# Two token halves of a norm, taken apart: the order of the products at the seams between stages

## What is computed

```
h = x + gate * (hidden @ w_down)                       # the product that ends a stage
u = h * rsqrt(mean(h * h, axis=-1) + eps) * g + shift  # one number per token
y = u @ w_next                                         # the product that begins the next stage
```

## Time and profile before

| what | before |
|---|---|
| median of 3 runs | 3476.15 us (3474.97 to 3476.59) |
| profiled execution, first to last instruction | 3472.8 us |
| TensorE busy | 3406.4 us, 98% |
| VectorE busy | 2199.6 us, 63% |
| ScalarE busy | 600.3 us, 17% |
| mean granted clock of TensorE | 0.996 |

### The profile page before, as it was taken

The page is one execution under the profiler, slowest core; times in us unless marked ns, Lnnn a source line. Parts: engine busy times, 40 slices in busy tenths (PEclk is TensorE's granted clock), DMA queues, the critical chain, the costliest instruction groups (busy, mean ns, idle before and its releaser), DMA issues.

```text
span 3472.8 us, 40732 instructions
## 1 busy us (share of the span) xinstructions
PE 3406.4 (98%) x16336; PEld 2811.9 (81%) x16336; DVE 2199.6 (63%) x4356; ACT 600.3 (17%) x1260; POOL 10.6 (0%) x12
## 2 busy tenths in 40 slices
PE   8999999999999999999999999999999999999999
PEld 6888867768888888888578888877688866888888
DVE  7776858767767677565356545554346567677754
ACT  2000023331000010001331000023411244012100
POOL 0000000000000000000000000010000000000000
PEclk9999999999999999999999999999999999999999
DMA  6433412213434434332112222222222211222222
GB/s 254 156 135 141 181 64 88 91 41 127 149 122 159 164 140 153 112 114 83 51 49 74 94 87 79 91 87 70 67 75 85 84 67 61 85 80 91 85 79 79
DMA packets 62083, 355.72 MB, mean 102 GB/s; under 512 B 6292, under 2 KB 15124, under 8 KB 32276
## 3 DMA queue, kind: packets, MB, share of 16 engines
q1 hardware_dynamic: 61895, 353.12, 29.2%
HBM read 350.83 MB, written 9.34 MB: 104 GB/s over the span
## 4 chain that ended last, share of the span: by engine, by line
PE 87%; DVE 9%; issue 2%; DMA 1%; ACT 1%; DVEq 0%; SPq 0%; ACTq 0%
PE turn L424 37%; PE lin L424 29%; PE lin L366 4%; PE lin L476 4%; PE turn L366 3%; PE score L1435 2%; PE out L1464 1%; PE lin L473 1%; DMA normed_T<-in_ada 1%; DVE work L823 1%; PE turn L1449 1%; PE out L424 1%; DVE work L2888 1%; DVE normed_sums L567 1%; PE turn L476 1%
## 5 line engine op out<-in xcount | busy, mean ns | idle before, releaser
L424 PE MATMUL turn<-normed_sums,weight_ring 128*128 128x256 f32 x3712 | 867.6, 379 | 0.4 <-DVE small L2907 0.4
L424 PEld LDWEIGHTS turn<-normed_sums,weight_ring 128*128 128x128 f32 x3712 | 705.0, 190 | 96.8 <-DVE small L2907 0.8
L424 PE MATMUL lin<-normed_T,weight_ring 128*128 128x256 f32 x2096 | 479.9, 380 | 1.2 <-ACT normed_T L779 1.2
L424 PEld LDWEIGHTS lin<-normed_T,weight_ring 128*128 128x128 f32 x2096 | 397.6, 190 | 58.8 <-issue 5.2
L503 DVE TENSOR_TENSOR products<-products,lin 128x512 f32<-128x512 f32 x182 | 125.1, 687 | 406.9 <-PE lin L424 378.8
L424 PE MATMUL turn<-arena,weight_ring 128*128 128x256 f32 x1618 | 371.3, 379 | 0.6 <-DVE arena L567 0.6
L424 PE MATMUL lin<-arena,weight_ring 128*128 128x256 f32 x1608 | 364.7, 380 | 2.0 <-DVE weight_ring L535 1.6
L424 PE MATMUL lin<-normed_sums,weight_ring 128*128 128x256 f32 x1432 | 345.5, 380 | 4.1 <-DVE normed_sums L567 4.1
L424 PEld LDWEIGHTS lin<-arena,weight_ring 128*128 128x128 f32 x1608 | 304.4, 190 | 45.8 <-DVE weight_ring L535 3.3
L424 PEld LDWEIGHTS turn<-arena,weight_ring 128*128 128x128 f32 x1618 | 306.6, 190 | 42.3 <-issue 1.0
L424 PEld LDWEIGHTS lin<-normed_sums,weight_ring 128*128 128x128 f32 x1432 | 270.9, 190 | 44.1 <-issue 6.2
(11 more groups left out here) (329 smaller groups left out, 3363.4 us busy)
## 6 DMA issues: line engine op xcount, KB each, us to landing
weight_ring<-in_up SPq DMA_DIRECT2D x110, 1024.0 KB, 4.8
arena<-in_ada SPq DMA_DIRECT2D x54, 768.0 KB, 4.4
weight_ring<-in_down SPq DMA_DIRECT2D x40, 1024.0 KB, 5.0
normed_T<-in_ada SPq DMA_DIRECT2D x36, 768.0 KB, 4.6
weight_ring<-in_down SPq DMA_DIRECT2D x20, 768.0 KB, 4.3
weight_ring<-in_dil_qk SPq DMA_DIRECT2D x9, 1024.0 KB, 5.0
weight_ring<-in_hyb_qk SPq DMA_DIRECT2D x8, 1024.0 KB, 4.8
weight_ring<-in_xbc SPq DMA_DIRECT2D x6, 1024.0 KB, 5.0
```

What stands on the lines that cost most here:

```text
L424: last = pe.matmul(o[:, n * H:(n + 1) * H], weight_block(slot, pairs, block, kp), op(kind, kp0 + kp), start=opens and n == 0 and kp == kps ...
```

## The change

The last slab's order becomes a, b, c (t3 alone), e (t4), d (t1, b22). With e the first token half is complete, and d, which only the second half needs, runs behind it; in a down projection the d of the second chunk is held back too (its slot with it) and runs just ahead of the last chunk's d. Between these products TensorE makes the sums and the spread of the first half's norm, each half with a bank of its own. The next stage takes its first two slabs together (`arriving_pair_pe`): the first half's products b11 and b21 of slab 0, then those of slab 1, then the rest of slab 0 pair by pair, then the rest of slab 1. Between the first ones it makes the sums and the spread of the second half. VectorE scales half tiles, first those of the first half (`normed_dve`), with the last three residual adds of the second half (`late_adds_dve`) after two of them behind an output projection and after all eight behind a down projection; then the second half and the operand sums (`second_half_dve`). ScalarE shifts half tiles (`normed_act`). The hybrid stage does the same with its first two projections, the last norm writes its result in 16 halves, and ffn0, which begins the kernel, keeps the old form. The keep-busy products at the seams go.

```diff
-        LAST_GROUPS = "abcde"
-        LAST_PRODUCTS = {"d": ((6, "b22"),), "e": ((3, "t4"),)}
+        LAST_GROUPS = "abce"
+        LAST_PRODUCTS = {"c": ((2, "t3"),), "e": ((3, "t4"),), "d": ((4, "t1"), (6, "b22"))}
...
+        PAIR_RINGS = ((0, 1, 0, 4), (2, 3, 4, 0), (1, 2, 3, 0))
+
+        def arriving_pair_pe(pe, c, op, beside):
+            there = halves_there(pe, c)
+            slots = [take_summed(pe, c), c.n["slab"] % SLOTS]
+            for n in range(2):
+                if n == 1:
+                    pe.wait_ge(slot_full[slots[1]], 16 * (c.n["slab"] // SLOTS + 1))
+                for b in PAIR_RINGS[n][:2]:
+                    after(pe, lin_taken[b], c[f"bank{b}"])
+                first, second = (lin[b][:, 0:H] for b in PAIR_RINGS[n][:2])
+                for kp in range(4):
+                    for o, block, kind in ((first, 0, "b11"), (second, 1, "b21")):
+                        there(kind, kp)
+                        last = pe.matmul(o, weight_block(slots[n], 4, block, kp), op(kind, kp), start=kp == 0, stop=kp == 3,
+                                         skip_group_check=True)
+                        if kp == 3 and kind == "b11":
+                            last.then_inc(lin_full[PAIR_RINGS[n][0]], 1)
+                        beside()
+            c.banks(*PAIR_RINGS[0])
+            job_done(c)
+            after(pe, lin_taken[0], c["bank0"])
+            after(pe, lin_taken[4], c["bank4"])
+            banks = {"b": lin[1], "c": lin[0], "d": lin[4]}
+            for kp in range(4):
+                for g, n, block, kind in (("b", 1, 5, "t2"), ("c", 0, 4, "t1"), ("c", 1, 2, "t3"), ("d", 0, 6, "b22"),
+                                          ("d", 1, 3, "t4")):
+                    weights_there(pe, c, block, kp)
+                    there(kind, kp)
+                    last = pe.matmul(banks[g][:, n * H:(n + 1) * H], weight_block(slots[0], 4, block, kp), op(kind, kp),
+                                     start=kp == 0 and n == 0 and g != "b", stop=kp == 3, skip_group_check=True)
+                    if kp == 3 and n == 1:
+                        bank_close(c, last)
+            halves_seen(c)
+            take_summed(pe, c)
+            c.banks(*PAIR_RINGS[1])
+            job_done(c)
+            for kp in range(4):
+                weights_there(pe, c, 5, kp)
+                last = pe.matmul(lin[3][:, H:T], weight_block(slots[1], 4, 5, kp), op("t2", kp), start=False, stop=kp == 3,
+                                 skip_group_check=True)
+            bank_close(c, last)
+            for g in "cd":
+                product_group(pe, c, slots[1], 4, g, op)
+            c.banks(*PAIR_RINGS[2])
...
+        def first_half_norm_pe(pe, c, final=False):
+            done = itertools.count(1)
+            def beside():
+                i = next(done)
+                if i == 3:
+                    tail_sum_pe(pe, c, 1, final)
+                elif final and i == 12:
+                    second_spread_pe(pe, 0)
+                elif not final and i == 6:
+                    spread_half_pe(pe, c, 0)
+            return beside
...
+        def second_half_norm_pe(pe, c):
+            done = itertools.count(1)
+            def beside():
+                i = next(done)
+                if i == 5:
+                    second_half_sums_pe(pe, c)
+                elif i == 8:
+                    spread_half_pe(pe, c, 1)
+            return beside
...
+        def late_adds_dve(v, c, inst):
+            b = c["late_bank"]
+            o = lin[b]
+            v.wait_ge(lin_full[b], c[f"bank{b}"])
+            v.wait_ge(dve_step, c["late"])
+            add_to_tail(v, inst, 7, 1, o[:, 0:H]).then_inc(tail_ready, 1)
+            vlink(v, c, add_to_tail(v, inst, 6, 1, o[:, 0:H]))
+            add_to_tail(v, inst, 6, 1, o[:, H:T]).then_inc(lin_taken[b], 1)
...
+        LATE_ADDS = {"slab": 2, "chunks": KT}
+        LATE_ROOT = {"slab": 6, "chunks": KT}
+
+        def normed_dve(v, c, prev, scale_half, ahead=4):
+            what, inst, sums_ahead = prev
+            reciprocal_dve(v, c, 0)
+            if sums_ahead:
+                weight_sums(v, c, 3)
+            half_there(v, c)
+            for k in range(KT + 1):
+                if k == LATE_ADDS[what]:
+                    late_adds_dve(v, c, inst)
+                if k == LATE_ROOT[what]:
+                    reciprocal_dve(v, c, 1)
+                if k < KT:
+                    scale_half(0, k)
+            half_there(v, c)
+            second_half_dve(v, c, lambda k: scale_half(1, k), ahead)
...
             for g in LAST_GROUPS:
-                if g == "d":
+                if g == "c":
                     tail_sums_start_pe(pe, c)
                 elif g == "e":
                     tail_sum_pe(pe, c, 0)
                 product_group(pe, c, slot, 4, g, op, last_slab=True)
-            tail_sums_pe(pe, c)
+            product_group(pe, c, slot, 4, "d", op, last_slab=True, beside=first_half_norm_pe(pe, c))
...
+            beside = first_half_norm_pe(pe, c, final)
+            last = product_group(pe, c, held, 4, "d", hidden_op, kp0=4, opens=False, closes=False, last_slab=True,
+                                 beside=beside)
+            last.then_inc(chunk_used, 1)
+            product_group(pe, c, slot, 3, "d", hidden_op, kp0=8, opens=False, last_slab=True, beside=beside)
```

More of the change, by code:

```diff
@@ L587, in tiles_seen, with halves_there, there, halves_seen @@
             c.add("sums", 3 * KT // 2)
+        def halves_there(pe, c):
+            tiles0, sums0 = c["u"], c["sums"]
+            def there(kind, kp):
+                if kind in ("b11", "b21"):
+                    pe.wait_ge(u_ready, tiles0 + 2 * kp + (1 if kind == "b11" else 2))
+                elif kind != "b22":
+                    pe.wait_ge(sums_made, sums0 + 3 * kp + {"t1": 1, "t3": 1, "t2": 2, "t4": 3}[kind])
+            return there
+        def halves_seen(c):
+            c.add("u", 2 * KT)
+            c.add("sums", 3 * KT // 2)
         u_pairs = in_pairs(uT)
@@ L631, in spread_half, with rinv_half, spread_half_pe @@
             return ins
+        rinv_bank = (outp[1], outp[0])
+        def rinv_half(h):
+            return rinv_bank[h][:, 0:H]
+        def spread_half_pe(pe, c, h):
+            c.add("spread")
+            pe.wait_ge(rinv_ready, c["spread"])
+            for b in range(2):
+                ins = pe.transpose(rinv_bank[h][:, b * P:(b + 1) * P], roots[h][:, b:b + 1].to_broadcast([P, P]), C("ident"))
+            ins.then_inc(rinv_spread, 1)
         def spread_pe(pe, c):
@@ L670, in tail_act, with late_squares_act, add_to_tail, sums @@
                 product_step_act(s, c, g)
[L671 to L678, removed]
-        def tail_dve(v, c, inst, ahead=True):
[L682 to L689, removed]
+            for n in range(2):
+                c.add("tail")
+                s.wait_ge(tail_ready, c["tail"])
+                tail_square_act(s, c, n, final)
+            root_act(s, c, 0)
+        def late_squares_act(s, c, final=False):
+            c.add("tail")
+            s.wait_ge(tail_ready, c["tail"])
+            tail_square_act(s, c, 2, final)
+            c.wait_mark(s, "blocks")
+            tail_square_act(s, c, 3, final)
+        def add_to_tail(v, inst, m, h, src):
+            tile = half(hT[:, m, :], h)
+            if inst is None:
+                return v.tensor_tensor(tile, src, tile, ALU.add)
+            return v.scalar_tensor_tensor(out=tile, in0=src, scalar=gate[:, inst, m:m + 1], in1=tile, op0=ALU.mult,
+                                          op1=ALU.add)
+        def tail_dve(v, c, inst, ahead=True):
+            def sums(stage):
                 if ahead:
-                    for stage in stages:
-                        weight_sums(v, c, stage)
+                    weight_sums(v, c, stage)
             job_done(c, note="p1_there")
@@ L775, in ada_norm_act, with ada_norm_dve, shift_half @@
+        def ada_norm_dve(v, c, inst, prev):
+            normed_dve(v, c, prev, lambda h, k: v.scalar_tensor_tensor(
+                out=half(uT[:, k, :], h), in0=half(hT[:, k, :], h), scalar=gs[:, inst, k:k + 1], in1=rinv_half(h),
+                op0=ALU.mult, op1=ALU.mult).then_inc(scaled, 1))
+        def ada_norm_act(s, c, inst, prev, first_copy=True):
             layer, sub = inst // 3, inst % 3
-            for k in range(KT):
+            def shift_half(h, k):
                 c.add("scaled")
@@ L778, in ada_norm_act @@
                 s.wait_ge(scaled, c["scaled"])
[L779 to L785 removed]
+                tile = half(uT[:, k, :], h)
@@ L2090, in mla_units, with mla @@
             return units
-        def mla():
+        def mla(prev):
             def sp(e, c):
-                for n in range(3):
-                    load_pair(e, c, a["mla_down"][n])
+                load_arriving_pair(e, c, a["mla_down"][0], a["mla_down"][1])
+                load_pair(e, c, a["mla_down"][2])
                 skip_jobs(c)
```

(14 more changed lines are left out.)

353 lines of the change are left out of this document (223 added, 130 removed).

## The result

The changed kernel takes 3489.98 us (median of 4 runs, 3488.07 to 3495.35) against 3475.56 us of the kernel before in the same comparison: a ratio of 1.0043 (95% interval 1.0031 to 1.0055). The forecast was 3475.0 with a range that ended at 3486. The profiled execution has a span of 3488.0 us and a time of its own of 3489.76, so some 1.8 us lie around the span, and its span is to be set against the 3472.8 us of the earlier trace rows: 15.2 us more.

A forecast was written before the change was run, and what follows sets the result against it. TensorE, busy 98% of the span, was taken as the bound, with only 68 us of seam losses open to change. Seam terms summed to -1.1 us: span 3471.7, plus 3.35 around it, 3475.0 us; range 3463 to 3486.

The forecast's parts named there:

- Moved products as cover: Seams: t1 and b22 run behind group e, 3.45 or 6.04 us of cover for the first half's norm, no product added.
- Late adds behind an output projection: Seams behind an output projection: TensorE stands 1.4 us for the third half tile, 1.2 for half tile 6; 5.0 lost.
- The wait for slab 1's weight sums: Six seams: TensorE stands 2.6 us until VectorE has made these sums inside slab 0's combination; 4.7 us in dilated.
- Rival 1: Slab 1's weight sums don't stop TensorE; 17.7 us of waits fall away: 3457 us. Chance 0.25 together with a half-way form.
- some 3 us more: Dilated, weight sums beside GpSimd's permutation: each of four could lose a whole copy, 1.35 us; not taken into the sum.
- Transfers: After a down projection slab 1 lands at t 9.3 and is asked for at 11.5: hidden, 2 us to spare.
- rival 3: Slab 1 comes late behind the held slot at ffn2, mla and dilated; 9 us more: 3484. Chance 0.05.
- TensorE ends its 14 products at 6.83 ... TensorE has done five products of the new slab at 8.99: Second half after a down projection: sums and spread end at 11.54 against 22 products, 9.50; 2.04 us lost.
- Rival 2: The clock falls at the six new waits, 1.7 us each, 10 us more: 3485. Chance 0.17.
- the prediction's own sign of being wrong: In the trace after, a granted clock under 1 beside the waits for weight sums would show the prediction wrong.
- with longer bubbles: Argument against a falling clock: five of the eight stretches at the old seams kept 1.00 with longer bubbles.
- Its terms for the end: Last seam: old chain 2.84 plus 8 x 0.67; new 0.79 inline, 3.7 from d's end, 8 x 0.39; given as -0.4.

The follow-up runs named there:

- experiment 3: Changed kernel with slab 1's weight sums placed right behind the operand sums, ahead of slab 0's combination, at the six paired seams: 3472.13 us, ratio 0.9986.
- Experiment 1: Changed kernel with one constant altered, the third PAIR_RINGS entry (1, 0, 2, 3) in place of (1, 2, 3, 0): 3483.86 us, ratio 1.0019.
- Experiment 2: Changed kernel with six products of no use added ahead of slab 1's t2, filling TensorE's stand: 3482.78 us, ratio 1.0020.

## Why the prediction was wrong

- **Moved products as cover: right.** The hybrid's seam, which has no pair of slabs, no weight sums and not the turned ring, gained 3.7 us for 4.0, and the end 0.2 for 0.4.
- **Late adds behind an output projection: right.** 2.24 us of stands at ffn1 for 1.4 + 1.2; the whole seam 9.3 for 9.1 at ffn3, 7.9 for 8.0 at the conv FFN.
- **The wait for slab 1's weight sums: right**, 17.2 us for 17.7, six times, the largest new wait. Rival 1 is out. In dilated it was 4.53 for 4.7, and the four sums took 0.98, 1.57, 0.98 and 1.24 us beside GpSimd's permutation, some 2 us more than alone. With the earlier sums of experiment 3 that wait is 0.78 us. The Trainium skill's page "SBUF — State Buffer" (section "SBUF: two separate sides"), by which the prediction priced some 3 us more, agrees in direction only; the term from the rows was the better one.
- **Transfers: right.** No wait for a landing of a slab; rival 3 is out.
- **"TensorE ends its 14 products at 6.83 ... TensorE has done five products of the new slab at 8.99": wrong.** This step let the new slab start as soon as the tiles were there and never asked which bank it opens. The late adds sat on that bank at three of seven seams, 1.5 to 1.8 us each, 4.9 in all. Experiment 1 showed it. The prediction followed the slots of the weight ring step by step and not the banks, though the diff has both.
- **The clock: named, priced right, and left out of the sum.** Rival 2 said 1.7 us a stand; measured were 1.65, 1.62, 1.69 and 2.44. It stood as an alternative with 0.17, yet the mechanism it needs, six stands on the path, was part of the likeliest case itself. It belonged into the sum, which put it at nothing; the prediction's own sign of being wrong, a granted clock under 1 beside the waits, came true at four of the six. With its 10 the forecast was 3485, with the bank as well 3490. That this meets the measured 3489.98 is in part luck, since the clock cost 7.4 and 2.8 us of the span's rise lie outside the seams. The argument against it, that five of the eight old seams kept 1.00 "with longer bubbles", took a seam's whole loss for one stand. In those five no single stand of TensorE was longer than 0.98 us, and three keep-busy products stood in each (six records, not six products). From the kernel before, its two longest kinds of wait in these seams, and the timeline of hybrid to ffn1:

```profile
PE lin L424 <- DVE normed_sums L567: 4.1, 7, 1.0
...
PE lin L366 <- ACT normed_T L779: 1.9, 3, 1.0
```

```profile
807.07 1.46 PE L371 MATMUL score<-constants 128*128 128x256 f32 x6
```

Experiment 2 showed that the idle stand is what costs the clock here: filled, it costs none. That the old keep-busy products go is not the cause by itself: experiment 3 has none of them either, and its t2 runs at full speed at all six seams.

Summed: -1.1 forecast, +4.9 bank, +7.4 clock make +11.2 of the 12.4 us found in the seams. The other 1.2, and the 2.8 outside, stay open.

Three slips in the prediction's sums changed nothing of this. Its terms for the end give -0.6 and not -0.4. The lower end of its own range is 3467 by its terms and not 3468. And the 3.35 us "around the span" set the span of one execution against the median of others; around a span lie 1.8.

## What to carry to other kernels

When work is moved ahead of a consumer, list for the first instruction behind it every resource that it opens, the accumulator bank as well as its operands: a rotated ring can put the last reader exactly there. A cover moved from one stand to another buys nothing until the work that it covers is moved too; here four VectorE operations, moved ahead of a combination, turned 0.4% lost into 0.1% won, and with the bank's order mended and the operations put where VectorE was idle it was 0.4% won. And a stand of TensorE costs its length and, at four of six seams here, also what then ran at 1.2 GHz behind it: if the sum contains the stand, it should contain a price for the clock.

## What the hardware showed beyond that

The granted clock fell behind stands of 2.54 us at three seams and not at two others of the same length in one execution, and in another kernel's at four of five; where six filler products took the stand's place it stayed at 1.00 in the stretches shown. Before the change five of eight seams kept 1.00, with no single stand above 0.98 us. But at the old seam from mla to ffn3 the clock fell (0.66 in the earlier trace rows) with no single stand above 0.34 us there, so the length of one stand doesn't settle it; what else does isn't shown here.
